# Who begins the stores of split weight slabs: SyncE, or GpSimd behind its own low parts

## The reference

```python
h = rmsnorm(x, g_mix)
a, gate, q, k, v = split(h @ w_in)            # 512, 512, 3 x 512 columns
u = a * sigmoid(gate)
c = silu(layernorm(causal_dwconv(u, w_dw) + b_dw)) @ w_pw
q, k = rmsnorm per head                        # 8 heads x 64
# stick-breaking: A[t,s] = beta[t,s] * prod_{s<j<t} (1 - beta[t,j]), s < t
x = x + concat(c, A @ v) @ w_out
f = relu(rmsnorm(x, g_ff) @ w_ff1)
x = x + (f * f) @ w_ff2                        # 4096 hidden
```

## Time and profile before

| | |
|---|---|
| median of 3 runs | 3025.5 us (3022.49 to 3030.76) |
| profiled execution, own time | 3021.44 us |
| its span in the trace | 3019.6 us |
| mean granted TensorE clock | 0.963 |
| DMA | 616.19 MB, 204 GB/s, one queue for all of the program's transfers |
| stores of split slabs | 94 of 1024 KB, 7.9 us from issue to landing (median) |

### The profile page before, as it was taken

One profiled execution on the slowest core, in us unless ns is written; L12 is line 12 of the kernel. 1 busy time (PEld: TensorE's weight loads), 2 busy tenths in 40 slices (PEclk: granted clock), 3 DMA queues, 4 the chain that ended last, 5 costly groups with the idle time before them and its releaser, 6 DMA issues.

```text
span 3019.6 us, 37393 instructions
## 1 busy us (share of the span) xinstructions
PE 2763.2 (92%) x13936; PEld 2296.0 (76%) x13936; DVE 1631.9 (54%) x2457; ACT 1084.2 (36%) x2177; POOL 754.6 (25%) x622
## 2 busy tenths in 40 slices
PE   6788767899999999999999998999999999999999
PEld 5565556667887787778888787777878877898887
DVE  4695664755666256637766355743777751212212
ACT  4223432345554212235555212232665640221121
POOL 4431334345554103112232002301333320000000
PEclk9899888899999999999999999999999999999999
DMA  8477566568765855755554844654544447253442
GB/s 295 173 241 264 160 227 235 218 233 294 253 237 201 349 207 202 262 205 188 172 171 151 324 184 152 226 195 178 177 160 163 147 161 286 112 195 140 168 167 88
DMA packets 262047, 616.19 MB, mean 204 GB/s; under 512 B 23217, under 2 KB 159409, under 8 KB 213741
## 3 DMA queue, kind: packets, MB, share of 16 engines
q1 hardware_dynamic: 261869, 613.80, 57.0%
HBM read 444.79 MB, written 168.94 MB: 203 GB/s over the span
## 4 chain that ended last, share of the span: by engine, by line
PE 63%; DVE 10%; ACT 4%; issue 3%; DMA 3%; POOL 3%; SPq 2%; ACTq 0%; DVEq 0%; POOLq 0%
PE ps L1891 8%; PE ps L1893 7%; PE ps L1892 7%; PE ps L2137 7%; PE ps L2138 7%; PE ps L2139 7%; DVE stay L1754 4%; PE ps L2109 3%; PE ps L2086 2%; PE ps L2078 2%; PE ps L2233 2%; PE ps L2235 2%; PE ps L2234 2%; POOL w_s L1022 2%; DVE cacc_second L1560 2%
## 5 line engine op out<-in xcount | busy, mean ns | idle before, releaser
L1108 POOL TENSOR_TENSOR beta<-beta,stay 128x512 f32<-128x512 f32 (+3 forms) x328 | 325.5, 994 | 732.6 <-DVE stay L1754 732.4
L1891 PE MATMUL ps<-h2T_hi,w_s 128*128 128x512 f32 (+1 forms) x1280 | 468.7, 366 | 7.2 <-DMA w_s<-w_scratch 3.0
L1892 PE MATMUL ps<-h2T_lo,w_s 128*128 128x512 f32 (+1 forms) x1280 | 456.1, 356 | 0.0
L1893 PE MATMUL ps<-h2T_hi,w_s 128*128 128x512 f32 (+1 forms) x1280 | 455.8, 356 | 0.0
L2137 PE MATMUL ps<-w_s,hid_hi 128*128 128x512 f32 (+1 forms) x1088 | 435.4, 400 | 12.6 <-DVE hid_lo L1825 12.6
L2138 PE MATMUL ps<-w_s,hid_lo 128*128 128x512 f32 (+1 forms) x1088 | 426.6, 392 | 0.0
L2139 PE MATMUL ps<-w_s,hid_hi 128*128 128x512 f32 (+1 forms) x1088 | 426.1, 392 | 0.0
L1825 DVE TENSOR_TENSOR hid_lo<-ps,hid_hi 128x512 fp32r<-128x512 f32 (+1 forms) x160 | 95.6, 598 | 474.1 <-ACT hid_hi L1464 474.1
L1382 ACT ACTIVATE stay<-ps 128x512 f32<-128x512 f32 (+3 forms) x328 | 173.4, 529 | 426.2 <-DVE ps L1742 217.5
L1022 POOL TENSOR_TENSOR w_s<-w_raw,w_s 128x1024 fp32r<-128x1024 f32 x94 | 242.3, 2599 | 274.0 <-ACT w_s L1165 274.0
L1820 DVE TENSOR_TENSOR resid<-ps,resid 128x512 f32<-128x512 f32 x256 | 174.4, 687 | 245.5 <-PE ps L2139 244.9
(11 more groups left out here) (195 smaller groups left out, 4975.2 us busy)
## 6 DMA issues: line engine op xcount, KB each, us to landing
w_s<-w_scratch SPq DMA_DIRECT2D x282, 1024.0 KB, 7.7
w_scratch<-w_s SPq DMA_DIRECT2D x94, 1024.0 KB, 7.9
w_raw<-in_w_ff SPq DMA_DIRECT2D x64, 512.0 KB, 5.1
a_k<-k_scratch SPq DMA_DIRECT2D x80, 256.0 KB, 3.9
a_v<-v_scratch SPq DMA_DIRECT2D x80, 256.0 KB, 4.1
a_q<-q_scratch SPq DMA_DIRECT2D x64, 256.0 KB, 4.4
w_raw<-in_w_in SPq DMA_DIRECT2D x20, 512.0 KB, 8.3
mix_scratch<-ohl SPq DMA_DIRECT2D x66, 128.0 KB, 2.5
```

What stands on the lines that cost most here:

```text
L1108: nc.gpsimd.tensor_tensor(v[0:q.r, 0:n], v[0:q.r, 0:n], stay[q.z % 3][0:q.r, 1:n + 1], ALU.mult).then_inc(s_a, 1)
L1891: nc.tensor.matmul(out, w[0], x[0], start=start, stop=False)
L1892: nc.tensor.matmul(out, w[0], x[1], start=False, stop=False)
L1893: return nc.tensor.matmul(out, w[1], x[0], start=False, stop=stop)
```

## The change

The 94 stores leave SyncE's list and its queue. GpSimd issues them, on its own DMA queue, at the end of `splits_until`: it waits for its own `lo_done` of that slab and begins the transfer. A store is due at `store_tick`, the same lag of 7 ticks behind the load (or the tick of the slot's next load), but GpSimd asks with the tick of the next slot (`tick + 2`), and never ahead of the split. SyncE's `weights` only loads. The semaphores `w_st` and all waits on them stay.

```diff
+def store_tick(n):
+    return min(load_tick(n) + STORE_LAG, load_tick(n + RING))
@@ SyncE
-            def store_slab(n):
-                kind, c, j = W[n]
-                sp.wait_ge(lo_done, FIRST[n] + 1)
-                sp.dma_start(w_d[W_ID[kind, j]], w_s[:, n % RING, :].bitcast(F32)).then_inc(w_st[n % RING], 16)
-
             def weights(t):
 
-                while True:
-                    n, i = at["load"], at["store"]
-                    if i < len(FIRST_ORDER):
-                        m = FIRST_ORDER[i]
-                        if m < n and (load_tick(m) + STORE_LAG <= t or (n < len(W) and m == n - RING and load_tick(n) <= t)):
-                            store_slab(m)
-                            at["store"] += 1
-                            continue
-                    if n < len(W) and load_tick(n) <= t:
-                        load_slab(n)
-                        at["load"] += 1
-                        continue
-                    return
+                while at["load"] < len(W) and load_tick(at["load"]) <= t:
+                    load_slab(at["load"])
+                    at["load"] += 1
@@ GpSimd
-            at = {"split": 0}
+            at = {"split": 0, "store": 0}
+
+            def store_slab(i):
+
+                n = FIRST_ORDER[i]
+                kind, c, j = W[n]
+                pool.wait_ge(lo_done, i + 1)
+                pool.dma_start(w_d[W_ID[kind, j]], w_s[:, n % RING, :].bitcast(F32)).then_inc(w_st[n % RING], 16)
@@ GpSimd, splits_until
                     at["split"] += 1
+                while at["store"] < at["split"] and store_tick(FIRST_ORDER[at["store"]]) <= t:
+                    store_slab(at["store"])
+                    at["store"] += 1
```

More of the change, by code:

```diff
@@ L655, in _ @@
             w2_k = w_ff2[0].rearrange("(k p) n -> p k n", p=P)
-            at = {"load": 0, "store": 0}
+            at = {"load": 0}
             def slab_source(kind, j):
```

## The result

The changed kernel takes 3060.4 us (median of 4 runs, 3053.3 to 3064.4) against 3024.8 us of the kernel before beside it on the same chip (4 runs): ratio 1.0112, 95% interval 1.0088 to 1.0136. The prediction was 3022 with a range to 3044, so it was wrong in sign and the time lies outside the range. The profiled execution took 3064.4 us, its span is 3062.6 (before 3019.6): 43.0 us to find, 7 more than the 36 between the medians.

What follows compares the result with a forecast made beforehand. The prediction took PE's chain as the bound, so only its waits for late results could be earned. Costs 5.1 less gains 8.3 gave -3.2 on 3021.4, so 3018.2; the runs' median stands 4.1 higher: 3022, range 3012 to 3044.

Steps and rivals of the forecast that it cites:

- The 104.6 us at L690: SP's 42 waits for low parts at the stores, removed by the change; SP's time, from which PE's waits don't follow.
- the same 16 DMA engines [...] move the same bytes: All stores: they go to another queue, but the same engines, 0.66 busy in window(0), carry them; no cost counted.
- Both are covered: SP's queue: 41 us of issues and 104.6 us of waits removed are hidden, as most loads behind wait for TensorE's slots.
- X: Price of one store issue on GpSimd: 1.1 us, bounds 0.44 and 2.5; 103 us for 94 stores.
- places 1 to 3: Store issues delaying GpSimd's root work in front (1.8 us) and out(0) (0.4), and beta products in window(0) (0.4).
- Rival B: GpSimd becomes the bound of attention through late beta products in window(0): middle 3040 us; chance 0.20.
- Place 4: End of window(0): last four stores begin only after the fourth low part, delaying everything behind; cost 2.5 us, bounds 0 and 5.
- The moved low parts: VectorE taps near 549 to 569 us and at 610 us meet fewer low parts; gain 7.1 us, bounds 0 and 10.
- only two of the four taps meet a low part: Four stores follow the fifth low part, so hid_lo comes at about 565.2 instead of 569.13; PE 3.9 us earlier.
- The gain of 1.2 us: Near 700 us, three raw f1 slabs no longer queue behind two stores; half of PE's 2.31 us pause, bounds 0 and 2.3.
- Rival D: An issue holds VectorE like a low part, or a store's bytes hold up raw loads: +8 us, 3033; chance 0.14.
- C: Freed queue and broken low-part runs are worth more, stores passing on their own queue: -14 us likely, 3012; chance 0.24.

Runs made afterwards that it cites:

- e0b_small: Kernel before, SyncE still storing, with GpSimd beginning a 64 KB transfer at each of the 94 store places: 3029.6 us, ratio 1.0020.
- e6_late: Changed kernel with stores 16 to 21 begun later, behind SyncE's v_scratch and q_scratch transfers: 3047.7 us, ratio 1.0073.
- e10_places: e6_late with five more stores moved in window(0): 50 behind mix_scratch<-pwo, 82 to 85 each right behind its low part: 3047.9 us, ratio 1.0079.
- e12_all: Changed kernel with the edits of e6_late, e10_places and e11_behind, and stores 90 to 93 each right behind its low part: 3042.8 us, ratio 1.0059.
- e7_eager: Changed kernel with twelve stores (22 to 25, 30 to 33, 90 to 93) each begun right behind its own low part: 3063.5 us, ratio 1.0127.
- e9_first16: GpSimd begins only the first 16 stores, four slots later than in the changed kernel; SyncE the other 78 as before: 3023.2 us, ratio 0.9994.
- e11_behind: e6_late with stores 34 to 39 begun behind the unbroken run of low parts at 567 to 587 us: 3043.0 us, ratio 1.0061.
- micro_share: Kernel before plus phases behind its end: a 512 KB load alone (4.0 us) or beside 4 MB of stores; phase b, stores begun by GpSimd: 11.9 us.
- e5_late2: Changed kernel with all of GpSimd's stores two slots of the schedule later: 3060.1 us, ratio 1.0120.
- e5_late4: Changed kernel with all of GpSimd's stores four slots of the schedule later: 3065.9 us, ratio 1.0138.
- e1_head: GpSimd begins the 30 stores before window(0), SyncE the 64 of window(0) as in the kernel before: 3039.9 us, ratio 1.0059.

## Why the prediction was wrong

**What bounds the kernel.** Right, and the point where the error began. The 104.6 us at L690 were SP's own time, and freeing them gained nothing. But the place on SP's list did a job the prediction didn't see: it kept the 94 stores in one line with everything else that SP begins.

**The step that failed** is in the paragraph on the rivals and in the one on what is removed: "the same 16 DMA engines [...] move the same bytes", taken as costing nothing, and "Both are covered". The bytes are the same, their order is not. There is no term for a transfer of SP's that finds stores ahead of it. By subtraction this term is at most about 30 of the 36 us: 36 less the 6 of e0b_small. The part that edits show is smaller: six stores moved win back 12.7 us of the time (e6_late; 15.3 us of PE's delay at 247 us), and 4.6 and 4.8 us go at two places of `window(0)` (e10_places), with new losses behind them; with 29 stores moved 18 us stay (e12_all). At 463 and 974 us the stores that come late and in a block of four cost 3.0 and 4.6 us (e7_eager), and there the cure of the first cost a later root. The rest is read from the traces, not separated. SP's waits for landings are little of it: 28.7 of the 44.9 us lie where nothing is lost, and e9_first16 has 50.4 us of them at no cost.

**X** was taken as 1.1 us and is 0.58, near the lower bound; places 1 to 3 would cost 0.1 us or less by the prediction's own sum. In e0b_small, which has the issues, PE loses nothing before 562 us, so that holds. Beside the sum the prediction put the Trainium skill's 1 us to the first byte in X's place; that is another quantity, and X, GpSimd's own time at an issue, is 0.58. Rival B (0.20) was refuted by its own sign: five waits for beta, 16.6 us.

**Place 4** was the only place where the prediction looked at when a store enters the engines, and there it was right in kind and too small: 2.5 us, bounds 0 and 5, against 4.6 from 974 to 1041 us, 2.4 of them in e0b_small too. The same reading at 174, 240, 473 and 700 us would have shown more of them. SP's timeline of the kernel before has the order of stores and small transfers.

**The moved low parts**, a gain of 7.1 us, became a loss of about 2.4 from 562 to 579 us. The step "only two of the four taps meet a low part" failed, since the tap that came up during the block of issues waited for them and for the low part behind them (5.2 us). The prediction named the condition, "that GpSimd at an issue does not hold up VectorE". The Trainium skill's rule from "SBUF — State Buffer", "Who interferes with whom", which spoke for the gain, agrees with the taps beside low parts and with e11_behind, where five taps beside issues alone took 0.74 us each. So the condition was met for issues by themselves; the rule does not settle the case that came, a tap held across issues with a low part behind.

**The gain of 1.2 us** for earlier raw slabs at 705 us came by less than half and was lost again. The three slabs land after 6.1 to 7.7 us (7.9 to 10.3 before), and the pause of 2.31 us is 1.83. But a `mix_scratch<-pwo` beside the stores takes 7.4 us instead of 2.7, ACT waits 8.3 us for it, and PE has a new pause of 2.70 us for `hid_lo` at 716 us.

**Rival D** was the nearest ("a store's bytes hold up the raw loads"), with 0.14 and a price of 8 us. Its first half is right for one tap, and its second half is the result, but at some four times that size and mostly for other transfers than the raw loads. C's argument, that a queue of its own lets stores pass, is refuted by micro_share: the load lands after 11.9, 11.1 and 10.5 us whichever queue has the stores.

The Trainium skill, page "DMA: Bandwidth & Descriptors", section "Queues, rings and completion order", says that each DMA engine goes round the queues that have work and changes only at packets. The traces agree with the taking of turns (265 packets against 267, 209 against 205). They differ on the packet, for which the page gives some 9 to 17 descriptors: in micro_share's phase b 16 store rows of 8 KB and 16 load rows of 512 bytes alternate every 0.33 us, one for one on the 16 engines, and the measurement decides. The same page's "Issuing engines are not separate DMA queues", used in the prediction against C, also agrees. Its other half, that more issuers save issue time only, was read as no harm; nothing in it promises that.

The delay of the first 174 us (-1.3 in the changed kernel, -3.3 in e5_late2, -4.3 in e5_late4, -0.7 in e9_first16) is not explained, and e1_head's 9 us behind 1041 us stay open too, as do most of the 18 us that e12_all still loses.

## What to carry to other kernels

A queue is also an order. Before a transfer moves to another engine's queue, list what the old queue began just behind and just ahead of it, and ask which of those small transfers will now find its bytes ahead of them. A long wait on the queue of an engine that computes nothing is not a reserve: here 104.6 us of it were worth nothing, and the order that came with it was worth 13 us for six stores, and for all of them at most some 30. An engine with idle time runs ahead of a schedule written in slots, so where a place matters its transfer needs a semaphore.

## What the runs showed of the hardware

- A transfer of 128 rows of 4 bytes is costly: 94 of them (48 KB in all) made the kernel 4.5% slower and took the landing of SP's 1 MB stores from a median of 7.9 to 17.7 us; with rows of 512 bytes, 128 times the bytes, the loss was 0.2%.
- GpSimd's issue takes 0.56 to 0.58 us for 512 bytes, for 64 KB and for 1 MB alike (128 rows each), and 0.75 us where each row goes to four places.
- Behind 4 MB of stores a 512 KB load in 512-byte packets lands after 10.5 to 11.9 us on any queue; in 4 KB packets after 9.1; begun 0.6 us ahead of the stores after 4.3. Two queues with work take turns row by row, 16 rows of 8 KB against 16 of 512 bytes in 0.33 us.
- A VectorE tap of 0.7 us took 5.2 us across three of GpSimd's DMA issues and the low part behind them; five taps beside issues with no low part behind took 0.74 us each.
